# Row spacing of 2112 bytes and halves of 256 and 264 tokens for the matmul inputs of a two-layer decoder step

## The chip, the cores and the metric

The kernel runs on one core of a Trainium2 chip. The time is that of the device, in microseconds, from one launch of the whole step; the median of three runs counts.

## The reference

One inference step of a small decoder trunk with model width 1024 and two layers, for a prompt of 512 tokens and eight sample requests of one token each. The 520 tokens share all weights, everything is fp32.

```python
for i in range(DEPTH):
    hp = hp + rmsnorm(mixer(rmsnorm(hp, g_pre_mix[i])), g_post_mix[i])
    u = rmsnorm(hp, g_pre_ffn[i]) @ ffn_w_up[i]        # 1024 -> 5632
    c = causal_conv3(u) + conv_b
    hp = hp + rmsnorm((silu(c[..., :2816]) * c[..., 2816:]) @ ffn_w_down[i], g_post_ffn[i])
    hp = hp + sigmoid(rmsnorm(hp, g_ple[i]) @ ple_w_gate[i]) * (p[i] @ ple_w_proj[i])
```

The mixer of layer 0 is an mLSTM (chunks of 64 tokens, 4 heads), that of layer 1 sliding-window attention (window 128, 16 heads, 4 of keys and values). The sample requests go through the same steps with their states and caches. Returned are the outputs, the new states, caches and convolution rows.

## The kernel before

**Layout.** Activations are held with features on the 128 partitions and the 520 tokens along them: a tensor of width 1024 is [128, 8, 520], one row of 520 tokens (2080 bytes) for each k, the block of 128 features. `h` is the residual.

**Products.** The matrix products run in fp32r, and each is made of three for precision. ACT rounds weights and inputs to a high part (`wH`, `xH`), DVE subtracts for the low part (`wL`, `xL`), and PE adds wH·xH, wH·xL and wL·xH in PSUM. The 520 tokens of an output tile don't fit a bank of 512 fp32, so each product is made of two halves of HT = 260 tokens: half q reads columns q·260 on, and writes columns 0 to 259 of bank q of the two-bank tile (lines 675 to 683):

```python
for n, (wt, xt) in enumerate(((wH, x[0]), (wH, x[1]), (wL, x[0]))):
    for q in range(2):
        mm = nc.tensor.matmul(out[:, q, 0:HT], wt[:, s, w], xt[:, k + x[2], q * HT:(q + 1) * HT],
```

A weight load of 128 x 128 goes before each product. A chunk is one output tile of 128 features: 8 k x 3 x 2 = 48 products, in a down stage 11 k and two chunks for each output tile.

**Stages.** Eleven stages follow each other (line 39): kv, qo, mout, up0, down0, ple0 for layer 0, and qkv, sout, up1, down1, ple1 for layer 1, with 13, 12, 8, 44, 16, 8, 12, 8, 44, 16 and 8 chunks. Inputs are `xH`, `xL` in most of them, `hidH`, `hidL` (22 rows) in the down stages, `pxH`, `pxL` (8 rows) and, for line 721, `pH`, `pL` (2 rows, 12 more products a chunk into `side`) in the embedding stages ple0 and ple1. Between the stages lie the mixers' own products (lines 761 to 1019), among them line 809, the outer product of the mLSTM's sample states: four fp32r products of 256 columns from `vmask` for each of eight requests.

**Order.** It is written out by hand with semaphores. SP streams weights chunk by chunk into two buffers `raw`, and waits only for `wL` two chunks before. For each chunk ACT makes `wH` (line 447) when PE is done with the chunk before the last, DVE makes `wL` (line 1030), and PE waits for `wL` and for the output tile to be read (two tiles alternate). DVE reads the finished tile with the normalisation factor (`scaled_read`, line 1090) or copies it (`copied`, line 1108), while PE is at the next chunk. ACT squares tiles for the norms (`squares`, line 504) and DVE multiplies `side` in the embedding stage (`add_embed`, line 1416). All four read two runs of 260 columns. Sums over features are fp32 products with a matrix of ones (lines 706, 747, 752) in halves of 260, and so is the rotation of line 905.

**Memory.** `Region` (lines 129 to 145) hands out addresses one after the other, each size rounded up to 32 bytes. The base is 16481, rounded up to 16512. The order is h, xH, xL, raw, wH, wL, u and so on; `arena` (line 187) is where the stages' own tensors begin, at 128064. xH lies at 33152, vmask at 192064.

Of the kernel before, what the change touches and what calls it, by code (L numbers as in the profile page):

```python
# [6 lines left out]
F32R = mybir.dt.float32r  # L7
ALU = mybir.AluOpType
# [4 lines left out]
P = 128  # L13
D = 1024
KT = D // P
SEQ, DEC = 512, 8
T = SEQ + DEC
HT = T // 2
NL = 2
EPS = 1e-6  # L20
NH, DV = 4, 256
# [7 lines left out]
FT = 22  # L29
UP = 2 * FT  # L30
DKH = FT // 2
EKT = 2
# [95 lines left out]
def build(nc, g):  # L128
    with ExitStack() as ctx:
# [23 lines left out]
            return ctx.enter_context(nc.psum_tensor(name, shape, F32))  # L153


        sb = Region((nc.sbuf_base + 31) // 32 * 32)
        h = sb("h", [P, KT, T])
        xH = sb("xH", [P, KT, T], F32R)
        xL_at = sb.top
        xL = sb("xL", [P, KT, T], F32R)  # L160
        raw = sb("raw", [P, 2, KMAX * P])
        wH = sb("wH", [P, 2, KMAX * P], F32R)
        wL = sb("wL", [P, 2, KMAX * P], F32R)
        u = sb("u", [P, 2, T + 2])
        cg = sb("cg", [P, T])
        cv = sb("cv", [P, T])
        sq = sb("sq", [P, 2, T])
        acc = sb("acc", [P, T])
        rstd = sb("rstd", [P, T])
# [14 lines left out]
        hot = const[:, C_HOT:C_HOT + NH * NH].rearrange("p (h m) -> p h m", h=NH)  # L184
        three = const[:, C_THREE:C_THREE + DEC]
        eye = const[:, C_EYE:C_EYE + DEC * DEC]
        arena = sb.top


        y_down = at("y_down", [P, KT, T], xL_at)  # L190
        ff = Region(arena)
        hidH = ff("hidH", [P, FT, T], F32R)
        hidL = ff("hidL", [P, FT, T], F32R)
        em = Region(arena)
        pxH = em("pxH", [P, KT, T], F32R)
        pxL = em("pxL", [P, KT, T], F32R)
        pin = em("pin", [P, EKT, T])
        pH = em("pH", [P, EKT, T], F32R)
        pL = em("pL", [P, EKT, T], F32R)
        ml = Region(arena)  # L200
        kvq = ml("kvq", [P, 4 * NH, T])
        y_ml = at("y_ml", [P, KT, T], ml.top)
# [54 lines left out]
        tile = [psum(f"tile{k}", [P, 2, 512]) for k in range(2)]  # L257
        sums = psum("sums", [P, 2, 512])
        side = psum("side", [P, 2, 512])
# [5 lines left out]
        s_mm, s_read = sem("chunk_done"), sem("tile_read")  # L265
# [3 lines left out]
        s_yc, s_dve, s_act = sem("y_copied"), sem("dve_step"), sem("act_step")  # L269
# [8 lines left out]
        s_sig, s_side = sem("sigmoid_done"), sem("side_read")  # L278
# [34 lines left out]
        def pslot(stage, k):  # L313
            return (TILE0[stage] + k) % 2

        def halves(ap):

            return ap.rearrange("p (q t) -> p q t", q=2)

        def following(stage):  # L320
            i = ORDER.index(stage) + 1
# [116 lines left out]
        def _(act):  # L438
# [51 lines left out]
            def squares(stage, by):  # L490


                def read(st):
                    if by == 2 and st.k % 2 == 0:
                        return
                    o, k = (st.pair, st.k // 2) if by == 2 else (st.at, st.k)
                    last = static(st) and k == KT - 1
                    if last:
                        act.wait_ge(s_mm, CHUNK0[stage] + COUNT[stage])
                    else:  # L500
                        act.wait_ge(s_yc, o(COPIED[stage] + 1))
                    if ON_DVE[stage] + k > 0:
                        act.wait_ge(s_acc, o(ON_DVE[stage]))
                    nc.scalar.activation(halves(sq[:, k % 2, :]), tile[pslot(stage, k)][:, :, 0:HT],
                                         ACT.Square).then_inc(s_last if last else s_read, 1)
                return read

# [166 lines left out]
        def _(pe):  # L674
            def product(stage, st, x, k, out, first, last):

                s = slot(stage, st.k)
                w = slice(k * P, k * P + P)
                for n, (wt, xt) in enumerate(((wH, x[0]), (wH, x[1]), (wL, x[0]))):
                    for q in range(2):  # L680
                        mm = nc.tensor.matmul(out[:, q, 0:HT], wt[:, s, w], xt[:, k + x[2], q * HT:(q + 1) * HT],  # L681
                                              start=first and n == 0, stop=last and n == 2)
                return mm

            def chunk(stage, st, x, fresh=False, direct=False):


                pe.wait_ge(s_low, st.at(CHUNK0[stage] + 1))
                down = stage[:4] == "down"
                o, k0 = (st.pair, st.k // 2) if down else (st.at, st.k)  # L690
                if TILE0[stage] + k0 >= 2 and not (down and st.k % 2):
                    pe.wait_ge(s_read, o(TILE0[stage] - 1))
                out = tile[pslot(stage, k0)]
                part = st.k % 2 if down else 0
                xs = (x[0], x[1], part * DKH) if down else (x[0], x[1], 0)
                if direct and NORM[stage]:
                    pe.wait_ge(s_root, NORM[stage])
                n = DKH if down else KT
                for k in range(n):
                    if fresh:  # L700
                        pe.wait_ge(s_xr, XSET[stage] + k + 1)
                    mm = product(stage, st, xs, k, out, k == 0 and part == 0, k == n - 1 and (not down or part == 1))
                    if direct:
                        pe.wait_ge(s_sq, ON_PE[stage] + k + 1)
                        for q in range(2):
                            ms = nc.tensor.matmul(sums[:, q, 0:HT], ones, sq[:, k % 2, q * HT:(q + 1) * HT],  # L706
                                                  start=(k == 0), stop=(k == KT - 1))
                        ms.then_inc(s_squ, 1)
                if stage[:3] == "ple":

                    done = KT * int(stage[3]) + st.k
                    if done or not static(st):
                        pe.wait_ge(s_side, st.at(KT * int(stage[3])))
                    if static(st) and st.k == 0:
                        pe.wait_ge(s_pr, int(stage[3]) + 1)
                    s = slot(stage, st.k)
                    for k in range(EKT):
                        w = slice((KT + k) * P, (KT + k + 1) * P)
                        for n, (wt, xt) in enumerate(((wH, pH), (wH, pL), (wL, pH))):
                            for q in range(2):  # L720
                                mm = nc.tensor.matmul(side[:, q, 0:HT], wt[:, s, w], xt[:, k, q * HT:(q + 1) * HT],  # L721
                                                      start=(k == 0 and n == 0), stop=(k == EKT - 1 and n == 2))
                mm.then_inc(s_mm, 1)

# [188 lines left out]
            for i in range(2):  # L913
                if i == 0:
                    pe.wait_ge(s_rope, 2 + KT)
                for b in range(NB):
                    mm = nc.tensor.transpose(side[:, i, b * P:b * P + P], vs[:, i, b * P:b * P + P], ident)
# [105 lines left out]
        def _(dve):  # L1023
# [63 lines left out]
            def scaled_read(stage, st, dst, rows=P):  # L1087

                dve.wait_ge(s_mm, st.at(CHUNK0[stage] + 1))
                nc.vector.tensor_tensor(halves(dst), tile[pslot(stage, st.k)][0:rows, :, 0:HT],  # L1090
                                        halves(rstd[0:rows, :]), ALU.mult).then_inc(s_read, 1)
                dve.wait_ge(s_read, st.at(TILE0[stage] + 1))

            def copied(stage, y, by):

                def mine(st):
                    return by == 1 or st.k % 2 == 1

                def is_last(st):
                    return static(st) and st.k == COUNT[stage] - 1  # L1100

                def first(st):
                    if mine(st):
                        o, k = (st.pair, st.k // 2) if by == 2 else (st.at, st.k)
                        dve.wait_ge(s_mm, st.at(CHUNK0[stage] + 1))
                        if is_last(st):
                            dve.wait_ge(s_last, sorted(COPIED.values()).index(COPIED[stage]) + 1)
                        nc.vector.tensor_scalar(  # L1108
                            y[:, bass.ds(o(), 1), :].rearrange("p o (q t) -> p (o q) t", q=2),
                            tile[pslot(stage, k)][:, :, 0:HT], 1.0, None, ALU.mult).then_inc(s_read if is_last(st) else s_yc, 1)  # L1110

                def then(st):
                    if mine(st) and not is_last(st):
                        o, k = (st.pair, st.k // 2) if by == 2 else (st.at, st.k)
                        dve.wait_ge(s_read, o(TILE0[stage] + 1))
                        dve.wait_ge(s_acc, o(ON_DVE[stage] + 1))
                        nc.vector.tensor_tensor(acc[:], acc[:], sq[:, k % 2, :], ALU.add).then_inc(s_acc, 1)
                return first, then
# [224 lines left out]
            def feed_forward(layer, mixer, y):  # L1343
# [68 lines left out]
                def add_embed(st):  # L1412

                    n = KT * layer
                    dve.wait_ge(s_sig, st.at(n + 1))
                    nc.vector.tensor_tensor(halves(cv[:]), halves(cg[:]), side[:, :, 0:HT], ALU.mult).then_inc(s_side, 1)
                    dve.wait_ge(s_side, st.at(n + 1))
                    o = bass.ds(st.at(), 1)
                    ht = h[:, o, :].rearrange("p o t -> p (o t)")
# [295 lines left out]
```

## Time and profile before

| | us |
|---|---|
| median of 3 runs | 1538.68 (1537.27 to 1543.86) |
| the profiled execution, its own time | 1543.55 |
| its span, first to last instruction | 1540.4 |
| PE busy in the span | 1435.6 |
| DVE busy | 903.1 |
| ACT busy | 507.7 |
| POOL busy | 31.3 |

The span is cut out of the execution's own time; what lies around it is 3.2 us. PE is the matmul engine and PEld its weight loads, which overlap it. A product's duration in the trace, 282 ns, is its latency: products are pipelined, and the next begins long before. What counts is the distance between the starts of two, the pitch, which has to be read from starts or from long unbroken pieces. A timeline row merges neighbours of one kind, so a row "x2" of 0.40 us is two products that overlap, and the distance to the next row's start is what the two cost. PEclk is the granted share of TensorE's clock: 1.00 is 2.4 GHz, 0.50 is 1.2 GHz.

### The profile page before, as it was taken

To read this page: it belongs to the slowest core of one execution; us is meant where nothing else is said; L and a number is where in the kernel's file an instruction comes from. 1 tells how busy PE (TensorE), PEld (TensorE's weight loads), DVE (VectorE), ACT (ScalarE), POOL (GpSimd) and SP (SyncE) were. 2 spreads that over 40 slices of the span, in tenths; PEclk is the share of its full clock that TensorE was granted. 3 is DMA by queue.
4 is the path that set the end of the run, shared out by engine and by line. 5 is a ranking of instruction groups with operands and counts; after the bars stand their busy time and mean duration, and the time that the engine had idled before them with its cause. 6 is when DMAs were issued, how large, how long until landed. Compare 5 with 4: busy or idle time off the path is not lost.

```text
span 1540.4 us, 27970 instructions
## 1 busy us (share of the span) xinstructions
PE 1435.6 (93%) x11049; PEld 1357.5 (88%) x11049; DVE 903.1 (59%) x1489; ACT 507.7 (33%) x804; POOL 31.3 (2%) x53
## 2 busy tenths in 40 slices
PE   6999999879999999999798988897999999999797
PEld 5989855779999999999698976696999999999797
DVE  4434543658777777232785565747777777523463
ACT  5121131235344344222422124634444344322241
POOL 2000100000000000000100010000000000000000
PEclk9999999889999999999899987998999999999999
DMA  6221520121222222322322220021222222322211
GB/s 205 84 82 56 191 110 0 53 82 55 95 84 93 95 85 100 112 85 82 119 94 69 82 87 1 1 69 42 95 89 88 95 92 85 119 94 86 89 52 72
DMA packets 32641, 129.90 MB, mean 84 GB/s; under 512 B 3960, under 2 KB 4048, under 8 KB 32064
## 3 DMA queue, kind: packets, MB, share of 16 engines
q1 hardware_dynamic: 27792, 110.36, 21.5%
q0 software_dynamic: 4800, 18.86, 3.4%
q8 instruction: 34, 0.56, 0.2%
q14 instruction: 15, 0.12, 0.0%
HBM read 120.57 MB, written 10.04 MB: 85 GB/s over the span
## 4 chain that ended last, share of the span: by engine, by line
PE 88%; DVE 8%; issue 2%; ACT 1%; DMA 0%; SPq 0%; POOL 0%; ACTq 0%; DVEq 0%
PE tile L681 75%; PE sums L706 3%; PE side L721 2%; PE side L854 1%; PE side L951 1%; DVE sm L1533 1%; DVE cg L1056 1%; PE sums L793 1%; DVE soft L1548 1%; PE tile L856 1%; PE tile L839 1%; PE side L905 1%; ACT wH L447 1%; PE sums L864 0%; PE side L882 0%
## 5 line engine op out<-in xcount | busy, mean ns | idle before, releaser
L681 PE MATMUL tile<-xH,wH 128*128 128x260 f32 x2256 | 466.4, 288 | 37.3 <-DVE xL L1060 32.0
L447 ACT ACTIVATE wH<-raw 128x1024 fp32r<-128x1024 f32 (+2 forms) x189 | 214.0, 1132 | 769.5 <-PE tile L681 713.4
L681 PE MATMUL tile<-xH,wL 128*128 128x260 f32 x2256 | 457.7, 285 | 0.0
L681 PE MATMUL tile<-xL,wH 128*128 128x260 f32 x2256 | 457.0, 284 | 0.0
L681 PEld LDWEIGHTS tile<-xH,wH 128*128 128x128 f32 x2256 | 354.0, 191 | 46.0 <-issue 40.3
L681 PEld LDWEIGHTS tile<-xH,wL 128*128 128x128 f32 x2256 | 351.0, 190 | 0.0
L681 PEld LDWEIGHTS tile<-xL,wH 128*128 128x128 f32 x2256 | 350.3, 190 | 0.0
L1030 DVE TENSOR_TENSOR wL<-raw,wH 128x1024 fp32r<-128x1024 f32 (+2 forms) x189 | 248.7, 1316 | 164.8 <-ACT wH L447 164.1
L681 PE MATMUL tile<-hidH,wH 128*128 128x260 f32 x704 | 142.1, 283 | 0.1
L681 PE MATMUL tile<-hidH,wL 128*128 128x260 f32 x704 | 141.5, 282 | 0.0
L681 PE MATMUL tile<-hidL,wH 128*128 128x260 f32 x704 | 141.4, 282 | 0.0
L1090 DVE TENSOR_TENSOR u<-tile,rstd 128x520 f32<-128x520 f32 x98 | 68.5, 699 | 99.4 <-PE tile L681 99.4
L681 PEld LDWEIGHTS tile<-hidH,wH 128*128 128x128 f32 x704 | 108.3, 188 | 0.4 <-issue 0.4
L681 PEld LDWEIGHTS tile<-hidL,wH 128*128 128x128 f32 x704 | 108.6, 188 | 0.0
L681 PEld LDWEIGHTS tile<-hidH,wL 128*128 128x128 f32 x704 | 108.4, 188 | 0.0
L681 PE MATMUL tile<-pxH,wH 128*128 128x260 f32 x256 | 55.7, 300 | 19.4 <-DVE pxL L1060 19.4
L1090 DVE TENSOR_TENSOR kvq<-tile,rstd 128x520 f32 (+1 forms) x24 | 16.8, 700 | 74.6 <-PE tile L681 74.5
L681 PEld LDWEIGHTS tile<-pxH,wH 128*128 128x128 f32 x256 | 41.5, 193 | 21.3 <-issue 20.2
L1108 DVE TENSOR_SCALAR y_down<-tile 128x520 f32 (+1 forms) x16 | 11.2, 700 | 81.9 <-PE tile L681 70.4
L681 PE MATMUL tile<-pxH,wL 128*128 128x260 f32 x256 | 52.6, 288 | 0.0
L681 PE MATMUL tile<-pxL,wH 128*128 128x260 f32 x256 | 52.5, 287 | 0.0
L706 PE MATMUL sums<-sq,const 128*128 128x260 f32 x160 | 47.3, 423 | 0.0
(264 smaller groups left out, 1506.9 us busy)
## 6 DMA issues: line engine op xcount, KB each, us to landing
raw<-in_w_up SPq DMA_DIRECT2D x88, 512.0 KB, 3.3
raw<-in_w_down SPq DMA_DIRECT2D x32, 704.0 KB, 4.1
raw<-in_w_ple SPq DMA_DIRECT2D x16, 640.0 KB, 3.9
raw<-in_w_kv SPq DMA_DIRECT2D x13, 512.0 KB, 3.3
raw<-in_w_qo SPq DMA_DIRECT2D x12, 512.0 KB, 3.3
raw<-in_w_qkv SPq DMA_DIRECT2D x12, 512.0 KB, 3.3
cring<-in_c_in POOLq DMA_DIRECT2D x8, 512.0 KB, 4.5
out_c_s<-cring POOLq DMA_DIRECT2D x8, 512.0 KB, 3.5
```

Of the source, the lines that this page charges most:

```text
L447: nc.scalar.activation(wH[:, k, 0:n], raw[:, k, 0:n], ACT.Copy).then_inc(s_high, 1)
L681: mm = nc.tensor.matmul(out[:, q, 0:HT], wt[:, s, w], xt[:, k + x[2], q * HT:(q + 1) * HT], start=first and n == 0, stop=last and n == 2)
L706: ms = nc.tensor.matmul(sums[:, q, 0:HT], ones, sq[:, k % 2, q * HT:(q + 1) * HT], start=(k == 0), stop=(k == KT - 1))
L721: mm = nc.tensor.matmul(side[:, q, 0:HT], wt[:, s, w], xt[:, k, q * HT:(q + 1) * HT], start=(k == 0 and n == 0), stop=(k == EKT - 1 and n ...
L793: mm = nc.tensor.matmul(sums[0:DEC, n // 2, (n % 2) * DV:(n % 2 + 1) * DV], qmask[:, b.k % 2, n, :], cring[:, b.k % 2, n, :], start=first ...
L839: mm = nc.tensor.matmul(out, kvq[:, n, j * P:j * P + P], kvq[:, 3 * NH + n, j * P:SEQ], start=True, stop=True)
L854: nc.tensor.matmul(side[:, half, j * P:SEQ], vtok[:, j, n, half * P:half * P + P], pj, start=(j == 0), stop=(j == NB - 1), skip_group_chec ...
L856: mm = nc.tensor.matmul(tile[1][0:NH, 1, j * P:SEQ], hot[:, n, :], pj, start=(n == 0 and j == 0), stop=(n == NH - 1 and j == NB - 1), skip ...
L905: mm = nc.tensor.matmul(side[:, q, 0:HT], perm, u[:, t.k % 2, q * HT:(q + 1) * HT], start=True, stop=True)
L951: mm = nc.tensor.transpose(side[:, c // 2, ((c % 2) * 2 + b) * P:((c % 2) * 2 + b + 1) * P], soft[:, gi % 2, c, b * P:b * P + P], ident)
L1030: nc.vector.tensor_tensor(wL[:, k, 0:n], raw[:, k, 0:n], wH[:, k, 0:n].bitcast(F32), ALU.subtract).then_inc(s_low, 1)
L1090: nc.vector.tensor_tensor(halves(dst), tile[pslot(stage, st.k)][0:rows, :, 0:HT], halves(rstd[0:rows, :]), ALU.mult).then_inc(s_read, 1)
```

## The change

Tensors that PE reads as moving operand in the products (`xH`, `xL`, `hidH`, `hidL`, `pxH`, `pxL`, `pH`, `pL`) get rows of TP = 528 tokens, 2112 bytes, of which 520 are used. The base of SBUF and `arena` are rounded up to 64 instead of 32, and `h` moves behind `wL`. The halves of lines 681 and 721 are 256 and 264 tokens (`cut`): the first goes to columns 256 to 511 of the lower bank, the second to columns 0 to 263 of the upper one, so that the 520 results lie side by side across the border of the banks, and the four readers take them in one run (`packed`). The fp32 products with ones, the rotation and their readers keep halves of 260.

```diff
+TA = 256
+TB = T - TA
+TP = 528
...
-        sb = Region((nc.sbuf_base + 31) // 32 * 32)
-        h = sb("h", [P, KT, T])
-        xH = sb("xH", [P, KT, T], F32R)
+        sb = Region((nc.sbuf_base + 63) // 64 * 64)
+        xH = sb("xH", [P, KT, TP], F32R)[:, :, 0:T]
         xL_at = sb.top
-        xL = sb("xL", [P, KT, T], F32R)
+        xL = sb("xL", [P, KT, TP], F32R)[:, :, 0:T]
...
         wL = sb("wL", [P, 2, KMAX * P], F32R)
+        h = sb("h", [P, KT, T])
...
-        arena = sb.top
+        arena = (sb.top + 63) // 64 * 64
...
-        hidH = ff("hidH", [P, FT, T], F32R)
+        hidH = ff("hidH", [P, FT, TP], F32R)[:, :, 0:T]
...
+        def packed(ap):
+
+            return ap.rearrange("p q t -> p (q t)")[:, TA:TA + T]
+
+        def cut(q):
+
+            return (slice(0, TA), slice(TA, T))[q], (slice(512 - TA, 512), slice(0, TB))[q]
...
-                        mm = nc.tensor.matmul(out[:, q, 0:HT], wt[:, s, w], xt[:, k + x[2], q * HT:(q + 1) * HT],
+                        mm = nc.tensor.matmul(out[:, q, cut(q)[1]], wt[:, s, w], xt[:, k + x[2], cut(q)[0]],
...
-                nc.vector.tensor_tensor(halves(dst), tile[pslot(stage, st.k)][0:rows, :, 0:HT],
-                                        halves(rstd[0:rows, :]), ALU.mult).then_inc(s_read, 1)
+                nc.vector.tensor_tensor(dst, packed(tile[pslot(stage, st.k)][0:rows]),
+                                        rstd[0:rows, :], ALU.mult).then_inc(s_read, 1)
```

`hidL`, `pxH`, `pxL`, `pH` and `pL` change as `hidH` does, line 721 as line 681, and lines 504, 1108 and 1416 as `scaled_read`.

## Rows read from the trace of the kernel before

**Rows 1.** The page: span, PE's busy time, and the chain that ended last.

```profile
span 1540.4 us, 27970 instructions
...
PE 1435.6 (93%) x11049; PEld 1357.5 (88%) x11049; DVE 903.1 (59%) x1489; ACT 507.7 (33%) x804; POOL 31.3 (2%) x53
...
PE 88%; DVE 8%; issue 2%; ACT 1%; DMA 0%; SPq 0%; POOL 0%; ACTq 0%; DVEq 0%
PE tile L681 75%; PE sums L706 3%; PE side L721 2%; PE side L854 1%; PE side L951 1%; DVE sm L1533 1%; DVE cg L1056 1%; PE sums L793 1%; DVE soft L1548 1%; PE tile L856 1%; PE tile L839 1%; PE side L905 1%; ACT wH L447 1%; PE sums L864 0%; PE side L882 0%
```

**Rows 2.** Chain in order of time: shares, then pieces (start us, us, what).

```profile
by line: PE tile L681 75.1%; PE sums L706 2.6%; issue 1.6%; PE side L721 1.5%; PE side L854 1.3%; PE side L951 1.1%; DVE sm L1533 1.0%; DVE cg L1056 0.9%; PE sums L793 0.8%; DVE soft L1548 0.8%; PE tile L856 0.7%; PE tile L839 0.6%; PE side
...
365.78 250.38 PE tile L681 x2082
...
616.19 119.15 PE tile L681 x990
```

**Rows 3.** Busy time by engine within stage up0; then PEclk, DMA share, GB/s.

```profile
core 0: us, PE busy (x) PEld busy (x) DVE busy (x) ACT busy (x) POOL busy (x), PEclk, DMA share, GB/s
...
366.00:615.00 249.00, 249.00 (x2074) 249.00 (x2074) 185.98 (x348) 104.23 (x154) 0.55 (x1) 1.00 0.27 91
```

**Rows 4.** Groups of instructions within 366 to 615 us (busy us, mean ns | idle).

```profile
L681 PE MATMUL tile<-xH,wH 128*128 128x260 f32 x672 | 135.3, 282 | 0.1
```

**Rows 5.** Groups by form, whole kernel: products of lines 681 and 721.

```profile
L681 PE MATMUL tile<-xH,wH 128*128 128x260 f32 x2256 | 466.4, 288 | 37.3 <-DVE xL L1060 32.0 <-DVE wL L1030 5.2
...
L681 PE MATMUL tile<-hidH,wH 128*128 128x260 f32 x704 | 142.1, 283 | 0.1
...
L681 PE MATMUL tile<-pxH,wH 128*128 128x260 f32 x256 | 55.7, 300 | 19.4 <-DVE pxL L1060 19.4
...
L721 PE MATMUL side<-pH,wH 128*128 128x260 f32 x64 | 13.1, 287 | 0.0
```

**Rows 6.** The same view: line 809, fp32r products of 256 columns.

```profile
L809 PE MATMUL side<-vmask,kst 72*128 72x256 f32 x32 | 5.1, 281 | 0.0
```

**Rows 7.** Timeline of PE, end of a qo chunk (start us, us, engine, what).

```profile
196.02 0.40 PE L681 MATMUL tile<-xH,wH 128*128 128x260 f32 x2
...
196.74 0.40 PE L681 MATMUL tile<-xH,wH 128*128 128x260 f32 x2
...
197.46 0.40 PE L681 MATMUL tile<-xH,wH 128*128 128x260 f32 x2
...
198.18 0.64 PE L809 MATMUL side<-vmask,kst 72*128 72x256 f32 x4
```

**Rows 8.** Windows, PE alone, at the start of ple0; last: PEclk, DMA.

```profile
747.44:748.30 0.86, 0.86 (x5) 0.50 0.95 398
```

**Rows 9.** Timeline of PE at the start of ple0.

```profile
746.87 0.77 PE L681 MATMUL tile<-pxH,wH 128*128 128x260 f32 x2 [9.71 <-DVE pxL L1060]
747.44 0.64 PE L681 MATMUL tile<-pxL,wH 128*128 128x260 f32 x2
747.87 0.64 PE L681 MATMUL tile<-pxH,wL 128*128 128x260 f32 x2
```

**Rows 10.** Groups by form on DVE: a read of PSUM, one of SBUF.

```profile
L1090 DVE TENSOR_TENSOR u<-tile,rstd 128x520 f32<-128x520 f32 x98 | 68.5, 699 | 99.4 <-PE tile L681 99.4
...
L1388 DVE TENSOR_TENSOR cv<-cg,cv 128x520 f32<-128x520 f32 x44 | 30.8, 701 | 4.6
```

**Rows 11.** Busy time by engine in stage ple0, columns as in rows 3.

```profile
770.00:812.00 42.00, 42.00 (x352) 42.00 (x351) 36.03 (x51) 10.70 (x12) 0.00 (x0) 1.00 0.28 99
```

**Rows 12.** Timeline of PE: transposes of 128 fp32 columns, four and one.

```profile
105.28 0.60 PE L771 MATMUL side<-const,kvq 128*128 128x128 f32 x4
...
108.23 0.27 PE L771 MATMUL side<-const,kvq 128*128 128x128 f32 x1
```

More of the change, by code:

```diff
@@ L186, in build @@
         eye = const[:, C_EYE:C_EYE + DEC * DEC]
-        arena = sb.top
+        arena = (sb.top + 63) // 64 * 64
         y_down = at("y_down", [P, KT, T], xL_at)
         ff = Region(arena)
-        hidH = ff("hidH", [P, FT, T], F32R)
-        hidL = ff("hidL", [P, FT, T], F32R)
+        hidH = ff("hidH", [P, FT, TP], F32R)[:, :, 0:T]
+        hidL = ff("hidL", [P, FT, TP], F32R)[:, :, 0:T]
         em = Region(arena)
-        pxH = em("pxH", [P, KT, T], F32R)
-        pxL = em("pxL", [P, KT, T], F32R)
+        pxH = em("pxH", [P, KT, TP], F32R)[:, :, 0:T]
+        pxL = em("pxL", [P, KT, TP], F32R)[:, :, 0:T]
         pin = em("pin", [P, EKT, T])
-        pH = em("pH", [P, EKT, T], F32R)
-        pL = em("pL", [P, EKT, T], F32R)
+        pH = em("pH", [P, EKT, TP], F32R)[:, :, 0:T]
+        pL = em("pL", [P, EKT, TP], F32R)[:, :, 0:T]
         ml = Region(arena)
@@ L503, in read @@
                         act.wait_ge(s_acc, o(ON_DVE[stage]))
-                    nc.scalar.activation(halves(sq[:, k % 2, :]), tile[pslot(stage, k)][:, :, 0:HT],
+                    nc.scalar.activation(sq[:, k % 2, :], packed(tile[pslot(stage, k)]),
                                          ACT.Square).then_inc(s_last if last else s_read, 1)
@@ L720, in chunk @@
                             for q in range(2):
-                                mm = nc.tensor.matmul(side[:, q, 0:HT], wt[:, s, w], xt[:, k, q * HT:(q + 1) * HT],
+                                mm = nc.tensor.matmul(side[:, q, cut(q)[1]], wt[:, s, w], xt[:, k, cut(q)[0]],
                                                       start=(k == 0 and n == 0), stop=(k == EKT - 1 and n == 2))
@@ L1108, in first @@
                         nc.vector.tensor_scalar(
-                            y[:, bass.ds(o(), 1), :].rearrange("p o (q t) -> p (o q) t", q=2),
-                            tile[pslot(stage, k)][:, :, 0:HT], 1.0, None, ALU.mult).then_inc(s_read if is_last(st) else s_yc, 1)
+                            y[:, bass.ds(o(), 1), :].rearrange("p o t -> p (o t)"),
+                            packed(tile[pslot(stage, k)]), 1.0, None, ALU.mult).then_inc(s_read if is_last(st) else s_yc, 1)
                 def then(st):
@@ L1415, in add_embed @@
                     dve.wait_ge(s_sig, st.at(n + 1))
-                    nc.vector.tensor_tensor(halves(cv[:]), halves(cg[:]), side[:, :, 0:HT], ALU.mult).then_inc(s_side, 1)
+                    nc.vector.tensor_tensor(cv[:], cg[:], packed(side), ALU.mult).then_inc(s_side, 1)
                     dve.wait_ge(s_side, st.at(n + 1))
```

## The prediction

> **What bounds the kernel now.** I read the page first. PE is busy 93% of a span of 1540.4 us, and PE holds 88% of the chain that ended last, 75% of it by the products of line 681 [rows 1]. Then the chain in order of time: both up and down stages of a layer stand in it as single PE pieces, the up stage as 2082 products in 250.38 us and the down stage as 990 in 119.15 us, with no piece of another engine between [rows 2]. Over a stretch of 249 us in that stage PE is busy for all of it at full granted clock, DVE for 186 us and ACT for 104 us [rows 3]. So in most of the kernel only one thing can change the time: the pitch from one product to the next. Loads, evacuations and splitting of weights lie beside it.
>
> The pitch: the up piece ends with one whole product (282 ns, [rows 4]), so its 2081 pitches take 250.38 - 0.28 = 250.10 us, 120.2 ns each. A product streams 260 columns; at 2.4 GHz that is 108.3 ns. So 11.9 ns of each pitch are not columns. Line 681 has 2256 + 704 + 256 products of one pairing of operands and as many of two others, 9648, line 721 has 3 x 64 = 192 [rows 5], 9840 in all; 9840 x 120.2 ns = 1183 us, and the chain gives these two lines 75.1% + 1.5% of 1540.4 us = 1180 us [rows 2]: every one counts in full. Whatever the change saves or costs per product is multiplied by 9840; per pair of halves, by 4920.
>
> **The change part by part.** Times are set against the profiled execution (1543.55 us, span 1540.4); the median of the runs, 1538.68, is 4.9 us or 0.3% below that, and I apply the difference to the median.
>
> *Halves of 256 and 264 columns.* The number of products, of weight loads and of columns stays: 520 columns a pair before and after. A row shows the 256-column product already. The products of line 809 are of the same type, read a tensor (vmask) that begins at byte 192064 = 3001 x 64 with rows of 1024 bytes, so each begins on a multiple of 64 and ends on one, and run in eight groups of four. 32 of them take 5.1 us busy and one 281 ns [rows 6]: a group takes 0.6375 us, three pitches and one product, so the pitch is (0.6375 - 0.281) / 3 = 118.8 ns; the rounding of 5.1 leaves 116.7 to 120.9. From 120.2 ns I would expect 4 / 2.4 = 1.7 ns less, 118.5. The two agree. So I take 118.5 for the half of 256 and, by the same slope, 120.2 + 1.7 = 121.9 for the half of 264: 240.4 ns a pair, as now. By the ends of the row the pair moves by -1.8 to +2.4 ns, that is -9 to +12 us.
>
> *Beginnings on multiples of 64.* By the allocator's arithmetic xH begins at byte 33152 = 518 x 64; a row of 2080 bytes is 32.5 x 64, a half 1040 bytes. So in every even k the first half begins on a multiple of 64 already, the second at 16 behind one; in odd k they begin at 32 and 48. The timeline shows the last three k of a chunk: k = 5 from 196.02 to 196.74, k = 6 to 197.46, k = 7 to 198.18 [rows 7]. Each takes 0.72 us for its six products, though three of the six in k = 6 begin on 64 and none in k = 5 or 7. The rows are rounded to 10 ns, so a beginning on 64 is worth at most 10 / 3 = 3.3 ns either way. Three quarters of the 9840 products get such a beginning anew: 7380 x 3.3 = 24 us at most, below or above. I take nothing, because the three triples are equal. The weight rows lay on multiples of 64 and still do, and the new row of 2112 bytes is 33 x 64.
>
> The Trainium skill (SBUF — State Buffer, Door 1: The DMA port swizzle) says that lines of SBUF are 16 bytes, and that accesses within one run at full bandwidth. Both 2080 and 1040 are multiples of 16, so by that page the old layout was aligned where it matters and the change gives nothing; the equal triples agree.
>
> *Half clock.* In the first products of the embedding stage the granted clock is 0.50, the level of 1.2 GHz, after a wait of 9.71 us; pairs begin 0.43 us apart [rows 8, 9], 217 ns a product, and 260 / 1.2 = 216.7. The excess of 11.9 ns is gone there. So it isn't a fixed price added to the columns; something beside the array takes about 120 ns and hides behind a slow array. Columns of a pair stay 520, so at half clock nothing changes either. What takes the 120 ns, the weight load or the read of the columns, is what the rivals differ in.
>
> *Results side by side.* The first half is written to columns 256 to 511 of the lower bank, the second to 0 to 263 of the upper one, and DVE and ACT read 520 columns in one run instead of two runs of 260. The read of two runs from PSUM takes 699 ns (line 1090), the same operation on one run in SBUF 701 ns (line 1388) [rows 10]: the break costs nothing now, so its removal saves nothing. A read across a bank border is in no row. Below: nothing gained. Above: double, 700 ns more. In the up stage DVE has 63 us idle of 249, 1.46 us a chunk of 43, and hides that. Exposed would be the last read of 11 stages, 7.7 us, and the embedding stage, where DVE is busy 36.0 of 42 us [rows 11], 6.2 of 7.2 us a chunk; two reads more make 7.6, 0.4 over, x 16 = 6 us. Together 14 us at worst. I take 0, since two runs and one run cost alike.
>
> *New addresses and larger rows.* h moves behind wL, 32 bytes are added a row, ACT and DVE write the same 520 contiguous columns of a row. No instruction, wait or transfer is added. Zero; the cover for all of it is the PE stretch with 25% idle DVE and 58% idle ACT [rows 3].
>
> Sum: 0 + 0 + 0 + 0, so 1538.7; I write 1539.
>
> **The rivals.** *Aligned reads run free (faster).* That the excess vanishes at half clock speaks for a bound on the side that feeds the array. Transposes of 128 fp32 columns, which pass twice (256 column passes), are 109 ns apart: four in 0.60 us with 273 ns for the last [rows 12]. If only the read's place made the 260-column product slower than that, the halves would take 109 and 112.4 ns, 221.4 a pair, 19.0 less; x 4920 = 93 us, 1445 us. A partial gain, by the bound above, would be up to 24 us. Against it: the 256-column product that begins and ends on 64 bytes still takes 118.8 ns, and equal triples. For it: that row has 72 rows of weights, not 128, so it is no perfect witness. I give 0.16 in all, 0.09 to the large one.
>
> The Trainium skill (TensorE: Matmul & The Clock Gate, Back-to-back issue gap) gives N / 2.4 + 2.5 ns for an isolated stream, 110.8 ns at 260. By that page 9.4 ns of each pitch is abnormal, and some repair could exist; the trace disagrees with it for this type and agrees for the transposes, so it names the prize of this rival but not its cause.
>
> *The pair becomes uneven (slower).* If the weight load sets a floor near 120.2 ns which 256 columns can't go below, while the 264 half, at the edge of it, pays for its four more columns, the pair is 120.2 + 121.9 = 242.1, 1.7 more; x 4920 = 8.3 us, 1547. It decides where the floor lies above 118.5, and the upper end of the line-809 pitch, 120.9, allows that. Against it: the row's middle. The chance is 0.15, and the read across the bank border is within its price.
>
> *It doesn't do what it says.* A base or a stride that leaves the rows off 64 would give the forecast's time. By the arithmetic it doesn't: every tensor ahead has a size that is a multiple of 64. It shares the forecast's time and changes nothing.
>
> **How the numbers follow.** No coupling to the place: 0.69, time 1539. Faster: 0.16. Slower: 0.15. A difference of 0.5%, 7.7 us or 0.8 ns a product, is about what a measurement of this kernel can tell from no change (the three runs shown lie within 0.43%). The range takes in -9 to +12 us of the row of line 809 cut to where most of it lies, with the uneven pair and the noise of 0.2% above, and part of the partial gain below: 1528 to 1549. The large gain, 0.09, and the ends of the partial gain and of the bank-border price lie outside.
>
> **What would show it.** Right: line 681 appears in two forms, 256 and 264 columns, the up stage's piece of the chain again at 250 us, pairs 0.24 us apart, group means of 282 ns for a product, the DVE read of a tile at 700 ns. The uneven pair: pieces of 252 us. Wrong: the up piece at 245 us or less, pairs at 0.22 to 0.23 us, with the embedding chunk shorter than 7.2 us; then the place of the read did hold the array back, and the row of line 809 was slow for another reason, its weights.

## The result and the profile after

| | before | changed |
|---|---|---|
| median, 18 runs each | 1542.80 us | 1546.85 us |
| range of the runs | 1536.74 to 1545.03 | 1542.35 to 1551.95 |
| ratio to before | | 1.0038 (1.0027 to 1.0049) |
| span of the profiled execution | 1540.4 us | 1544.4 us |

The changed kernel is slower by 0.26 to 0.38%: the medians lie 4.05 us apart, the ratio on record says 0.38%, 5.9 us, with an interval from 4.2 to 7.6 us. That is clear of no change and below the 0.5% that the prediction took for a difference. The page after the change, with the lines that answer to [rows 1] and, in its fifth part, the read of a tile:

```profile
span 1544.4 us, 27970 instructions
...
PE 1443.3 (93%) x11049; PEld 1364.6 (88%) x11049; DVE 903.3 (58%) x1489; ACT 508.7 (33%) x804; POOL 31.4 (2%) x53
...
PE tile L692 76%; PE sums L717 3%; PE side L732 2%; PE side L865 1%; PE side L962 1%; DVE sm L1544 1%; DVE cg L1067 1%; PE sums L804 1%; DVE soft L1559 1%; PE tile L867 1%; PE tile L850 1%; PE side L916 1%; PE sums L875 0%; PE side L893 0%; PE sums L1011 0%
...
L1101 DVE TENSOR_TENSOR u<-tile,rstd 128x520 f32<-128x520 f32 x98 | 68.6, 700 | 104.4 <-PE tile L692 104.4
```

PE's busy time grew by 7.7 us, with the same number of instructions; DVE's by 0.2 and ACT's by 1.0. The read of 520 results in one run across the border of the banks takes 700 ns, against 699 in two runs [rows 10]. The pieces of the chain, which answer to [rows 2] (start us, us, what):

```profile
360.27 258.62 PE tile L692 x2130
618.92 119.04 PE tile L692 x990
...
1077.72 258.62 PE tile L692 x2130
1336.38 119.05 PE tile L692 x990
```

The up piece now holds 2130 products, one chunk more than before, so it has to be read per product: (258.62 - 0.28) / 2129 = 121.34 ns, against 120.18. The down piece stands at (119.04 - 0.28) / 989 = 120.08, against 120.19. So the time was lost outside the down stages, although all stages got the same halves and the same row. The starts in the trace give it to a nanosecond: an undisturbed chunk of 48 products in kv, qo, mout, up0, qkv, sout and up1 took 5766.7 ns and takes 5826.7, 60 ns more, and so does a chunk of the embedding stages (60 products, 7200 and 7260 ns); two down chunks of 66 took 15.85 us and take 15.84.

The timeline shows seven pairs in the up stage, after the change (start us, us, engine, what):

```profile
400.07 0.41 PE L692 MATMUL tile<-xH,wL 128*128 128x256 f32 x2
400.31 0.41 PE L692 MATMUL tile<-xH,wH 128*128 128x256 f32 x2
400.56 0.40 PE L692 MATMUL tile<-xL,wH 128*128 128x256 f32 x2
400.80 0.41 PE L692 MATMUL tile<-xH,wL 128*128 128x256 f32 x2
401.05 0.40 PE L692 MATMUL tile<-xH,wH 128*128 128x256 f32 x2
401.29 0.40 PE L692 MATMUL tile<-xL,wH 128*128 128x256 f32 x2
401.53 0.41 PE L692 MATMUL tile<-xH,wL 128*128 128x256 f32 x2
```

Pairs are 0.24 or 0.25 us apart where they were 0.24. The loss is in the flow of the products and not in a wait between chunks.

By the starts, the first down stage begins 2.7 us later than before, the second 4.8 us later, the end is 4.0 us later. That is less than the products lost in their flow, for the first chunks of the stages, which follow a wait, took different times in the two executions. The changed kernel was 1.6 us ahead when qo began, and 0.9 us when the first up stage did. Its first weights landed in 6.48 us and not 6.74, and it left the slow pace at the very start (pairs 0.43 us apart, where PEclk says 1.00 all the same) one k sooner, as the second piece of six products shows (first the changed kernel's, then the one of before, by the same view):

```profile
16.11 0.72 PE tile L692 x6
```

```profile
16.38 1.27 PE tile L681 x6
```

Between 46 and 52 us it had the full clock and the kernel before a granted share of 0.82 (window, PE busy, PEclk, DMA share, GB/s; again the changed kernel first), and one chunk of kv took 5.90 us in place of 7.24:

```profile
46.00:52.00 6.00, 6.00 (x52) 1.00 0.37 134
```

```profile
46.00:52.00 6.00, 6.00 (x44) 0.82 0.54 178
```

This is not the change's doing: between 46 and 52 us the kernel with padding alone has 0.81 and the one with even halves side by side 1.00. So I count the steady chunks by themselves. Without the first three distances between chunks of each stage (four in kv), the starts of the changed kernel add up to 6.7 us more than those of before: 4.8 in the two up stages, 0.5 in the two embedding stages, 0.2 less in the two down stages, the rest in the others. The three or four at the beginning of each stage add up to 2.2 us less.

### The profile page after: what moved, and what is told of

Same layout as the page of the kernel before. It is cut to its first block, busy times and chain, and to the rows that moved or that the text cites. A ratio compares the mean times of both kernels' runs of the same rounds, so it can differ in the third digit from the quotient of the medians.

```text
span 1544.4 us, 27970 instructions
## 1 busy us (share of the span) xinstructions
PE 1443.3 (93%) x11049; PEld 1364.6 (88%) x11049; DVE 903.3 (58%) x1489; ACT 508.7 (33%) x804; POOL 31.4 (2%) x53
## 4 chain that ended last, share of the span: by engine, by line
PE 89%; DVE 7%; issue 1%; ACT 1%; DMA 0%; SPq 0%; POOL 0%; ACTq 0%; DVEq 0%
PE tile L692 76%; PE sums L717 3%; PE side L732 2%; PE side L865 1%; PE side L962 1%; DVE sm L1544 1%; DVE cg L1067 1%; PE sums L804 1%; DVE soft L1559 1%; PE tile L867 1%; PE tile L850 1%; PE side L916 1%; PE sums L875 0%; PE side L893 0%; PE sums L1011 0%
## 5 line engine op out<-in xcount | busy, mean ns | idle before, releaser
L692 PE MATMUL tile<-xH,wH 128*128 128x256 f32 x2256 | 469.8, 290 | 35.4 <-DVE xL L1071 31.7
L692 PE MATMUL tile<-xH,wL 128*128 128x256 f32 x2256 | 461.5, 286 | 0.0
L692 PE MATMUL tile<-xL,wH 128*128 128x256 f32 x2256 | 458.5, 285 | 0.0
L692 PEld LDWEIGHTS tile<-xH,wH 128*128 128x128 f32 x2256 | 359.1, 191 | 43.8 <-issue 38.5
L692 PE MATMUL tile<-hidH,wH 128*128 128x256 f32 x704 | 142.0, 283 | 0.1
L692 PE MATMUL tile<-hidL,wH 128*128 128x256 f32 x704 | 141.8, 283 | 0.0
L692 PE MATMUL tile<-hidH,wL 128*128 128x256 f32 x704 | 141.8, 283 | 0.0
L692 PE MATMUL tile<-pxH,wH 128*128 128x256 f32 (+1 forms) x256 | 55.7, 299 | 19.4 <-DVE pxL L1071 19.4
L692 PE MATMUL tile<-pxH,wL 128*128 128x256 f32 (+1 forms) x256 | 52.5, 287 | 0.0
L692 PE MATMUL tile<-pxL,wH 128*128 128x256 f32 (+1 forms) x256 | 52.2, 285 | 0.0
```

The costliest lines, as they stand in the source:

```text
L692: mm = nc.tensor.matmul(out[:, q, cut(q)[1]], wt[:, s, w], xt[:, k + x[2], cut(q)[0]], start=first and n == 0, stop=last and n == 2)
```

## The experiments

The first four kernels part the change into its pieces and test what sets the pitch.

**Padding alone.** Rows of 2112 bytes, base and arena on 64, h behind wL; halves of 260 in the lower columns of each bank, two runs in the reads. Against the changed kernel:

```diff
-                        mm = nc.tensor.matmul(out[:, q, cut(q)[1]], wt[:, s, w], xt[:, k + x[2], cut(q)[0]],
+                        mm = nc.tensor.matmul(out[:, q, 0:HT], wt[:, s, w], xt[:, k + x[2], q * HT:(q + 1) * HT],
...
-                nc.vector.tensor_tensor(dst, packed(tile[pslot(stage, st.k)][0:rows]),
-                                        rstd[0:rows, :], ALU.mult).then_inc(s_read, 1)
+                nc.vector.tensor_tensor(halves(dst), tile[pslot(stage, st.k)][0:rows, :, 0:HT],
+                                        halves(rstd[0:rows, :]), ALU.mult).then_inc(s_read, 1)
```

> Only the rows of 2112 bytes, the base on 64 and the move of h; halves of 260 in the lower columns of both banks, as before. Theory F (a floor of about 120 ns that the weight load sets, and columns that cost only above it): the pair stays at 240.3 ns, the up piece of the chain at 120.2 ns a product, ratio 1.000. Theory P (the place of rows and weights decides): the pair is as in the changed kernel, 242.7 ns, 121.3 ns a product in the up piece, ratio 1.004.

Ratio 0.9989 (0.9979 to 0.9998). The up piece of its chain:

```profile
362.92 250.10 PE tile L682 x2082
```

120.05 ns a product. The new row costs nothing by itself; if anything it gains 0.1%. In its kv stage, with the same addresses, a steady chunk takes 5733 ns (119.4 ns a product) in place of the 5760 of its up stages; I come back to that.

**Uneven halves alone.** The changed kernel with rows of 2080 bytes.

```diff
-TP = 528
+TP = T
```

> Only the halves of 256 and 264 and the results side by side; rows of 2080 bytes. Theory F: as the changed kernel, 121.3 ns a product in the up piece, ratio 1.004. Theory P: as before, 120.2 ns, ratio 1.000.

Ratio 0.9989 (0.9977 to 1.0). Its up piece:

```profile
359.95 256.17 PE tile L692 x2130
```

120.19 ns a product. xL lies 16640 = 65 x 256 bytes behind xH here, as in the kernel before. The uneven halves cost nothing by themselves either. Theory F had laid the loss on this part and theory P on the padding, and both fell: each part is free alone, together they cost 0.38%.

**Halves of 240 and 280.**

```diff
-TA = 256
+TA = 240
...
-            return ap.rearrange("p q t -> p (q t)")[:, TA:TA + T]
+            return ap.rearrange("p q t -> p (q t)")[:, 512 - TA:512 - TA + T]
```

> The changed kernel with halves of 240 and 280 tokens instead of 256 and 264 (begins on multiples of 64 bytes too). Theory F with the slope of the columns above the floor: 240 columns stay at 120 ns, 280 take 280/2.4 + 11.9 = 128.6 ns, the pair 248.6, 8 ns more than before, x 4920 = 40 us, ratio about 1.026. No floor, a fixed 11.9 ns behind each product: 111.9 + 128.6 = 240.5, ratio 1.000. A floor alone, with columns at 109 ns to 119 ns beneath it: 240, ratio 1.000.

Ratio 1.0074 (1.0058 to 1.009). Its up and down stages are one piece:

```profile
361.12 378.76 PE tile L692 x3120
```

(378.76 - 0.28) / 3119 = 121.35 ns, a pair of 242.7 ns as with 256 and 264, and none of the values that were expected. The starts in the trace give 111.5 ns behind the short and 131 ns behind the long half. A floor of 120 ns under each product is thus refuted: 240 columns go below it by what they lack. In its down stage a pair takes 242.0, not 240 as in the changed kernel, which adds to the loss.

**Narrow weights.** The kernel before, with 64 columns of weights in the products with the low parts, which are left out for the upper half of the output rows.

```diff
+                        rows = P if n == 0 or last and n == 2 else HD
+                        w = slice(k * P, k * P + rows)
-                        mm = nc.tensor.matmul(out[:, q, 0:HT], wt[:, s, w], xt[:, k + x[2], q * HT:(q + 1) * HT],
+                        mm = nc.tensor.matmul(out[0:rows, q, 0:HT], wt[:, s, w], xt[:, k + x[2], q * HT:(q + 1) * HT],
```

> The kernel before with 64 columns of weights instead of 128 in the second and third product of each k (wH x xL, wL x xH), but for the last of an output tile: the low parts are left out for half of the output rows. Columns of tokens and their places are as before. Theory F: four of six products lose the floor of their weight load and fall to about 111 ns, the mean to 114, x 9840 = about 60 us less, ratio 0.96. If the read of the columns sets the pitch: 120.2 ns, ratio 1.000.

Ratio 0.9924 (0.9906 to 0.9941), not 0.96. Two groups of weight loads of its up stage (busy us, mean ns), and the up piece of its chain:

```profile
L683 PEld LDWEIGHTS tile<-xH,wH 128*128 128x128 f32 x644 | 99.0, 188 | 0.0
L683 PEld LDWEIGHTS tile<-xL,wH 128*64 128x64 f32 x643 | 81.3, 134 | 0.0
```

```profile
363.87 248.37 PE tile L683 x2082
```

A weight load of 64 columns takes 134 ns in place of 188, and the pitch is (248.37 - 0.28) / 2081 = 119.22 ns in place of 120.18. In four products of six the load is 54 ns shorter, and that buys 1 ns. The weight load does not set the pitch of 260 columns, and theory F, which was the mechanism of the prediction's slower rival, is gone.

Four more ask where the 60 ns a chunk come from.

**Even halves side by side.** The changed kernel with 260 and 260, results in columns 252 to 511 and 0 to 259.

```diff
-TA = 256
+TA = 260
...
-            return ap.rearrange("p q t -> p (q t)")[:, TA:TA + T]
+            return ap.rearrange("p q t -> p (q t)")[:, 512 - TA:512 - TA + T]
```

> The changed kernel with halves of 260 and 260: rows of 2112 bytes, results still side by side (columns 252 to 511 and 0 to 259), read in one run. If the place in PSUM or the read across the bank border costs the 60 ns a chunk that padding alone and uneven halves alone did not: up pieces at 121.4 ns a product, ratio 1.004. If it takes uneven halves and padded rows together: 120.0 ns, as with padding alone, ratio 0.999.

Ratio 0.9954 (0.9936 to 0.9972, four runs): faster than both kernels. The pieces of its two up stages:

```profile
360.94 248.98 PE tile L692 x2082
...
1076.74 250.10 PE tile L692 x2082
```

119.51 and 120.05 ns. So neither the place in PSUM nor the single read across the banks costs anything; it takes uneven halves and padded rows together. The same code ran at two pitches in two layers. They are two patterns of the flow, that is, of the distances from start to start, which repeat chunk after chunk. In up0 the six products of k = 0 to 3 take 726, 707, 722 and 713 ns, in up1 719, 723, 720 and 717, with every address the same; and padding alone ran its kv stage in the first of these patterns and its up stages in the second.

**Weights 64 and 128 bytes further.**

```diff
+        sb.top += 64
         wH = sb("wH", [P, 2, KMAX * P], F32R)
```

and the same with 128.

> The changed kernel with 64 unused bytes ahead of wH: weights (and all behind them, hidH and hidL too) lie 64 bytes further from xH and xL, everything still on multiples of 64. Theory P (the place of rows and weights relative to each other, within 256 bytes, decides): the up stage leaves 121.4 ns a product, most likely towards 120.0, and the down stage, whose rows move with the weights, stays at 120.0; ratio near 1.000. Theory C (the columns alone, 256 and 264, in stages of 8 k): unchanged, 121.4 ns, ratio 1.004.

> The same with 128 unused bytes. Theory P: a third value in the up stage, the down stage at 120.0. Theory C: 121.4 ns, ratio 1.004.

Ratios 1.0036 (1.0021 to 1.0051) and 1.0034 (1.0022 to 1.0047). The up piece of the one and of the other:

```profile
360.48 258.66 PE tile L693 x2130
```

```profile
365.75 252.91 PE tile L693 x2082
```

121.36 and 121.40 ns. Theory P, as I had put it, fails: the distance to the weights leaves the sum alone. But the starts show that this distance is felt. In the changed kernel the six products of k = 0 to 3 of a chunk of the up stage take 729, 719, 731 and 734 ns, and k = 4 to 7 the same four again. With the weights 64 bytes further they take 734, 729, 719 and 731, with 128 bytes 731, 734, 729 and 719: the pattern turns by one k for each 64 bytes. (In the kernel before, with rows of 2080 bytes, the eight k take 716, 719, 717, 741, 723, 718, 722 and 710 ns.) A row of 2112 bytes moves 64 bytes from k to k within 256, a k of weights (512 bytes) not at all; so each distance within 256 comes up twice in 8 k, and a shift changes only the order. In these two kernels hidH, pxH and their low parts move with the weights.

**Everything 32 bytes further.** No half begins on a multiple of 64 any more. For xH, xL and the weights all distances stay. For the tensors of `arena` they don't, though the expectation says so: in the changed kernel `sb.top` is 128576, a multiple of 64, so the edit moves `arena` to 128672, by 96 bytes, and hidH, hidL, pxH and pxL lie 64 bytes further from the weights.

```diff
-        sb = Region((nc.sbuf_base + 63) // 64 * 64)
+        sb = Region((nc.sbuf_base + 63) // 64 * 64 + 32)
...
-        arena = (sb.top + 63) // 64 * 64
+        arena = (sb.top + 63) // 64 * 64 + 32
```

> The changed kernel with every tensor 32 bytes further: all distances as in the changed kernel, but no half begins on a multiple of 64 any more. Theory P: the up stage at 121.4 and the down stage at 120.0, ratio 1.004. If beginnings on multiples of 64 matter by themselves, either way, both stages move by the same amount a product.

Ratio 1.0033 (1.002 to 1.0045), and in its chain:

```profile
360.39 258.63 PE tile L692 x2130
619.05 119.03 PE tile L692 x990
```

121.35 and 120.08 ns, as in the changed kernel. For what the up stages read, nothing but the beginnings changed, so whether a half begins on a multiple of 64 does not matter there; this is the plainest answer to what the change was built on.

The embedding stages did move. Two chunks of the first one, in the changed kernel and then in this one (48 of the 60 products each, so the distance of the two starts is a whole chunk, 7.26 and 7.18 us):

```profile
787.57 5.82 PE tile L692 x48
794.83 5.82 PE tile L692 x48
```

```profile
788.31 5.75 PE tile L692 x48
795.49 5.75 PE tile L692 x48
```

By the starts a chunk takes 7187 ns in both embedding stages, 73 less than in the changed kernel and 13 less than before: 119.8 ns a product, with halves of 256 and 264, rows of 2112 bytes and pxL at the same place within 256 bytes as pxH. Either the 64 bytes between these rows and the weights did it, or the beginnings; no run separates the two.

In the changed kernel, what differed between the stages that lost and those that didn't is the distance of high and low rows. xL lies 16896 = 66 x 256 bytes behind xH, and pxL as far behind pxH: the same place within 256 bytes. hidL lies 46464 = 181.5 x 256 behind hidH, 128 bytes apart within 256, and the down stages lost nothing. That became theory D, and the last four kernels test it and measure the columns.

**Low parts 128 bytes apart.**

```diff
         xH = sb("xH", [P, KT, TP], F32R)[:, :, 0:T]
+        sb.top += 128
...
         pxH = em("pxH", [P, KT, TP], F32R)[:, :, 0:T]
+        em.top += 128
```

> The changed kernel with 128 unused bytes between xH and xL and between pxH and pxL, so that high and low rows lie 128 apart within 256 bytes in every stage, as hidH and hidL do already; halves of 256 and 264 on multiples of 64. Theory D (with uneven halves, high and low rows at the same place within 256 bytes cost 1.4 ns a product): up and the other stages of 8 k fall from 121.4 to 120.0 ns a product, about 8 us less than the changed kernel, ratio to before 0.998 to 1.000. If the columns alone do it: 121.4 ns, ratio 1.004.

Ratio 1.0003 (0.999 to 1.0016). Its pieces:

```profile
363.57 250.09 PE tile L694 x2082
613.71 119.06 PE tile L694 x990
...
1079.06 250.09 PE tile L694 x2082
```

120.04 ns in the up stages, with halves of 256 and 264 and rows of 2112 bytes. A chunk takes 5760 ns, 67 less than in the changed kernel. The weights move with xL here; moving them alone did nothing, so it is the distance between xH and xL. With that the loss of the stages that read xH and xL is accounted for.

**Low parts 64 bytes apart**, the first of the two edits alone, with 64.

> The same with 64 unused bytes between xH and xL alone. Theory D: the up stage moves off 121.4 ns, to 120.0 or between; the embedding stages stay. If the columns alone do it: 121.4 ns, ratio 1.004.

Ratio 0.9975 (0.9962 to 0.9988), better than before. Its up piece:

```profile
362.55 248.97 PE tile L693 x2082
```

119.51 ns; a chunk takes 5733 ns, in every stage that reads xH and xL. Its pattern no longer repeats after four k: in the first up stage the eight k take 708, 710, 708, 718, 726, 723, 718 and 722 ns. The embedding stages, which it leaves alone, keep their pair of 242.0 ns, where the kernel with 128 bytes apart has 240.2. So each stage follows the distances of its own rows. Which distance it is in the embedding stages is less clear than in the others: the kernel with everything 32 bytes further had 239.6 there with high and low rows at the same place, and the edit with 128 bytes moved pH and pL as well.

**Even halves and low parts 128 bytes apart.** Both edits on the kernel with even halves.

> Halves of 260 side by side in rows of 2112 bytes, and high and low rows 128 apart. Theory D says nothing is left to gain with even halves: up stage at 119.4 to 120.0 ns a product, ratio 0.995 to 0.999, as without the 128 bytes.

Ratio 0.9993 (0.9981 to 1.0006), 120.0 ns in both up stages: nothing gained over padding alone. It also does not enter the 119.5 that the even halves without the 128 bytes showed in one layer.

**Halves of 128 and 392.**

> The changed kernel with halves of 128 and 392. It measures what the excess over N/2.4 is made of. A fixed 11.9 ns a product: 392 columns take 175 ns. In proportion to the columns (120/260 ns each): 181 ns. The short half can't go below its weight load, about 110 ns by the transposes. Pair 285 or 291 ns instead of 240, ratio about 1.14 or 1.16; the 6 ns between the two are read from the piece of the chain of an up stage.

Ratio 1.1599 (1.1575 to 1.1623). Its up and down stages are one piece, and four pairs of the timeline follow:

```profile
398.58 452.61 PE tile L692 x3120
```

```profile
500.22 0.45 PE L692 MATMUL tile<-xH,wH 128*128 128x128 f32 x2
500.51 0.45 PE L692 MATMUL tile<-xL,wH 128*128 128x128 f32 x2
500.80 0.45 PE L692 MATMUL tile<-xH,wL 128*128 128x128 f32 x2
501.09 0.45 PE L692 MATMUL tile<-xH,wH 128*128 128x128 f32 x2
```

(452.61 - 0.45) / 3119 = 145.0 ns a product, a pair of 290 ns. The expectation took 109 ns for the short half [rows 12], which would leave 181 for 392 columns, in proportion to 120 / 260. The starts don't bear that split out. In the up stages the long half begins 58 ns after the short one, and the next short one 232 ns after the long. So 128 columns do not take 109 ns from start to start, and 392 take far more than 181. The pair alone comes out near one of the two expected values, but that does not show what the excess is made of. In the range of 256 to 264 columns the pitches of even and uneven halves (118.4, 120.1 and 121.9 ns) fit 120 / 260 ns a column and N / 2.4 + 11.8 ns alike, each within 0.3 ns.

## Why the prediction was right, and where its reasons were not

**The sum.** The forecast was 1539, no difference to a median of 1538.7; the measured ratio is 1.0038. It is inside the range and inside "within 0.5%", but it is not zero. The measured median of 1546.85 lies near the upper end of the range, 1549; 4.1 us of the distance to the forecast are there because the kernel before ran at 1542.80 in these runs, and are not the change's. The step that failed is the first one, the pair of halves: I had 118.5 + 121.9 = 240.4 ns, and in the stages of 8 k it is 2 x 121.34 = 242.7, in the down stages 240.2. In even halves of the same padded rows the pair is 240.1. Each column count by itself was priced well: with rows of 2080 bytes the starts give 118.4 ns and 121.9 ns in the up stage. What was missing is that two terms which I added up, halves and rows, are not independent. No row of before could show that, since no stage of before had both. That the answer "no difference" held within 0.5% is in part luck: the interaction came to 2.3 ns a pair and left out the down stages, and the working has no bound for it.

The size fits: the steady chunks add up to 6.7 us, and the ratio says 4.2 to 7.6. In qo and qkv, where other products come between, a part of it does not appear: a late chunk of qo took 8267 ns and takes 8273.

**Beginnings on multiples of 64.** Nothing taken, up to 24 us as bound. Right in the result: the kernel with everything moved by 32 bytes has the up and down pieces of the changed one. The equal triples [rows 7] were a weaker witness than I took them for. By the starts those three took 719, 721 and 711 ns, which the rounding hid, and in the up stage k = 3, which the rows don't show, takes 741. A triple is no pure measure of where its halves begin; the pattern over k was there to be seen in the kernel before. The statement of the Trainium skill that lines of SBUF are 16 bytes (SBUF — State Buffer, Door 1: The DMA port swizzle) spoke against a gain from 64, and no run here contradicts it; but it would also let one expect that offsets in multiples of 64 change nothing, and the pitch here follows distances of 64 and 128 within 256. The measurement decides.

**Half clock.** No difference expected. The first k of ple0, after the change and at PEclk 0.50, bears it out (timeline of PE, then the window):

```profile
749.49 0.78 PE L692 MATMUL tile<-pxH,wH 128*128 128x256 f32 x2 [9.70 <-DVE pxL L1071]
750.07 0.64 PE L692 MATMUL tile<-pxL,wH 128*128 128x256 f32 x2
750.50 0.64 PE L692 MATMUL tile<-pxH,wL 128*128 128x256 f32 x2
```

```profile
749.90:750.90 1.00, 1.00 (x6) 0.50 0.92 383
```

From its first start to that of the product with ones behind it, its six products take 1.44 us, as they did before [rows 9], and the second and third pair begin 0.43 us apart in both.

**Results side by side.** Taken as 0, bound 14 us. Right: 700 ns against 699 for the read, and the kernel with even halves side by side is no slower than the one with padding alone.

**The rivals.** The aligned read that runs free got 0.16 and did not come: 93 us were never there. Its price took the transposes' 109 ns for 128 columns as 256 column passes; the rows give the time, not the passes. The uneven pair got 0.15, with 120.2 + 121.9 = 242.1 ns and 8.3 us; the up stages came out at 242.7 ns, so its figure was nearer than the forecast's, and the 8.3 us nearer to the 6.7 of the steady chunks than none. Its mechanism is wrong all the same. It rested on a floor from the weight load, and 240 columns at 111.5 ns and weight loads shortened by 54 ns for 1 ns of pitch leave no such floor at 120. In the kernel with 128 and 392 the starts have 58 ns behind the short half. A number near the right one for a wrong reason would have misled the next step: the remedy would have been even halves, where it is as well a shift of xL by 128 bytes.

**The witness.** Line 809 was my best row, and it was read rightly: 118.8 ns for 256 columns, 119.0 by the starts, and 118.4 for the half of 256 with rows of 2080 bytes. I took it for a property of the product, and it isn't one. In the changed kernel the same four products (line 820 there) read vmask at the same place within 256 bytes, with the same code, and their starts are 124, 128 and 117 ns apart, to 1 ns in all eight groups: 123.0 on average. With halves of 260 side by side or of 240 and 280, and the same addresses, they are at 119.5 and 119.7. They read one moving tensor, so what slows them is not a distance between two tensors of their own. A row taken from one flow of products is no safe price for another.

**Left open.** Why uneven halves, padded rows and an equal place of xH and xL within 256 bytes meet in this way is not shown; that moving xL by 64 or 128 bytes takes the loss away is, in all stages that read xH and xL. For the embedding stages even the condition is open, since they ran at 119.8 ns with an equal place once. Why the same code with the same addresses runs in one stage at 119.5 and in another at 120.0 (even halves, and padding alone) is open as well; uneven halves showed one value in all undisturbed stages of a kernel that read xH and xL. The ratio of 0.9954 of the even halves side by side, 7 us, is more than that can explain: its steady chunks are 1.8 us shorter than before, and in its profiled execution the other 3 us and more came from first chunks in kv and qo, which differ between executions of the other kernels too. There are four runs; whether they share this is not shown.

## What to carry to other kernels

When PE is busy throughout, price a layout change per product and multiply by their number: here 1 ns is 10 us. Then test the parts of the change alone before adding their prices, since two edits that are each free can cost together when both move the addresses of one stream. And if a stage loses time that its neighbour with the same edit doesn't, compare how far apart their operands lie before looking for a wait: here 64 or 128 unused bytes between two tensors took back all of the loss of the stages that read them. When an edit moves a base that is rounded up further on, work out the addresses of all tensors: 32 bytes at the start were 96 behind the rounding, and the embedding stages changed their pitch.

## What the runs showed of the hardware

- At 2.4 GHz, fp32r products of 256 to 264 columns with a weight load each flow about 12 ns slower than N / 2.4, 120 ns for 260 columns, whatever their start (multiples of 16, 32 or 64 bytes). Whether the 12 ns are fixed or grow with the columns is not shown. At half clock the excess is gone, 217 ns for 260 [rows 8, 9]. The Trainium skill (TensorE: Matmul & The Clock Gate, Back-to-back issue gap) gives N / 2.4 + 2.5 ns for the isolated gap, an estimate of 110.8 ns at 260 columns. The same section says that in a stream both the weight loads and the products set the spacing, so it is no figure for such a stream, as which the prediction used it; the up stages here never averaged less than 119.2 ns at 260 columns.
- A weight load of 64 columns took 134 ns in the trace, one of 128 took 188; with the shorter one in four products of six the pitch fell by 1 ns.
- The flow of products depends on addresses within 256 bytes. In the stages of 8 k with halves of 256 and 264 and rows of 2112 bytes it turned by one k for each 64 bytes between rows and weights, and a product took 121.4 ns with the high and low rows at distance 0, 119.5 at 64 and 120.0 at 128. In the embedding stages it was 121.0 ns at distance 0 and 119.8 at distance 0 with rows and weights 64 bytes further apart and every beginning off the multiples of 64.
- Addresses alone don't fix the flow: with even halves in the same padded rows, stages with equal addresses ran at 119.5 or 120.0 ns, and four products whose code and place within 256 bytes stayed ran at 119.0 ns before and 123.0 after the change.
- A VectorE read of 520 fp32 in one run across the border of two PSUM banks takes the same 700 ns as two runs of 260.
